# Root columns of five norms spread by one-pass products of high and low halves, in a two-layer diffusion block on one core

## The chip, the cores and the metric

The kernel runs on one core of a Trainium2 chip. The metric is the device time of one execution in microseconds (us). TensorE (PE) multiplies, and its weight loads (PEld) run beside its products. VectorE (DVE), ScalarE (ACT) and GpSimd (POOL) work elementwise, and SyncE (SP) issues the transfers (DMA).

## The reference

The input is 512 latent tokens and 256 context tokens of width 1024, all in float32. Two layers follow each other; each has a mixer (layer 0: Fourier groups and neighbourhood attention, layer 1: differential attention) and a squared-ReLU MLP of 4096 hidden units. Ahead of each of these four sub-layers, and once at the end, stands an RMS norm:

```
def rms_norm(x, g, eps=NORM_EPS):
    xf = x.astype(jnp.float32)
    y = xf * lax.rsqrt(jnp.mean(xf * xf, axis=-1, keepdims=True) + eps)
    return (y * g.astype(jnp.float32)).astype(x.dtype)

def modulate(x, g, shift, scale):
    return rms_norm(x, g) * (1.0 + scale) + shift
```

Shift, scale and gate come from the products of a condition vector with `w_mod` (1024 x 6144 for each layer).

## The kernel before, in words

Activations lie transposed: the 1024 features are 8 tiles of 128 partitions, the 768 tokens run along the free axis. Weights stream in as units of 128 x 1024 float32; ACT rounds each to float32r (`w_hi`, line 784), POOL makes the rest (`w_lo`, line 625), and PE takes every product as three one-pass products of halves: low by high, high by low, high by high (lines 1713 to 1715). The order of the work on each engine is written out by hand, and semaphores tie the engines together.

**A norm.** There are five, numbered i = 0 to 4, and each has two parts j: for i = 0, 1 and 2 the 512 latent tokens and the 256 context tokens, for i = 3 and 4 two halves of 256 latent tokens. ACT squares the features, DVE adds the eight tiles into `ssum`. `norm_sums` on PE (line 1764) sums `ssum` over the partitions, with `ssum` as weights and a column of ones, so that the sums stand as columns: one token for each partition, one column for each 128 tokens. ACT takes the square root into `stat` (line 822). `norm_root` on DVE takes the reciprocal (line 1280), and for each of the two or four columns writes a diagonal, `ident` times the column, into `diag` (line 1282). `norm_spread` on PE multiplies `diag` by a float32 matrix of ones (line 1771, one instruction in the source and two records in the trace), which leaves the row of roots, the same on all 128 partitions, in bank 6 + j. DVE multiplies it into the activations (line 1306), ACT and DVE make the high and low half of `h` (lines 836 and 1315), or ACT and POOL (line 643) for part 1.

**Where the spreads stand on PE.** For i = 1 to 4, part 0 is spread between two half units of the last projection (`tail`), part 1 for i = 1 to 3 inside the first three units of the next projection (`first_three`), and part 1 of i = 4 after the last product of the kernel; behind it come only the copy of the row, the last scaling and the output's transfers.

**The head.** PE starts with `hold(PAD, 7)`: 46 products of a float32r tile of ones with 512 columns of ones, whose result nobody reads. Then it works through this list, in order:

```
            half_mm(0)
            ...
            hold(3, 7)
            half_turn(0)
            ...
            norm_sums(0, 0)
            norm_sums(0, 1)
            half_mm(1)
            norm_spread(0, 0)
            norm_spread(0, 1)
            half_turn(1)
            hold(HOLD, 5)
            head_three(0, [(0, 0), (0, 1), (1, 0), (1, 1)])
```

`half_mm(m)` multiplies 512 modulation columns (`mod_big`, line 1918), each half of it after its own transfer; `half_turn(m)` turns the result into columns (line 1942), from which DVE makes the scale that the first `h` needs (lines 1474 and 1255). `head_three` are the first products of the projection. SP waits for the whole first `h` before it issues the next loads of weights.

Of the kernel before, what the change touches and what calls it, by code (L numbers as in the profile page):

```python
# [19 lines left out]
F32 = mybir.dt.float32  # L20
F32R = mybir.dt.float32r
ALU = mybir.AluOpType
# [3 lines left out]
P = 128  # L26
# [3 lines left out]
TOK = LAT + CTX  # L30
NT = TOK // P
# [28 lines left out]
MOD_VS = [2, 1, 1]  # L60
HPAIRS = HEADS // 2
HOLD = 12
PAD = 46
NTILES = HPAIRS * NT


# [20 lines left out]
def build(nc, t):  # L87

    ctx = ExitStack()
    with ctx:  # L90
        base = 16512

        def at(name, shape, dt, offset):
            return nc.alloc_sbuf_tensor_at(name, shape, dt, offset=offset)

        size = lambda *shape: int(np.prod(shape)) * 4
# [9 lines left out]
        scr = rest + 2 * size(TOK, KT)  # L106
# [9 lines left out]
        c_off = [con_at]  # L116

        def const(name, shape, dt=F32):
            o = c_off[0]
            c_off[0] += (size(*shape[1:]) + 31) // 32 * 32  # L120
            assert c_off[0] <= rest
            return at(name, shape, dt, o)

        ident = const("ident", [P, P])
        ones_r = const("ones", [P, P], F32R)
# [4 lines left out]
        cond = const("cond", [P, KT, 2])  # L130
        cact = const("cact", [P, KT, 2])
        eps_c = const("eps_c", [P, 2])
        stat = const("stat", [P, 64])
        modr = const("modr", [P, 2, 4])
        dft_at = c_off[0]
        dft_hi = const("dft_hi", [P, 256], F32R)
# [22 lines left out]
        tmp_a = at("tmp_a", [P, 2, TOK], F32, scr)  # L159
        tmp_b = at("tmp_b", [P, 2, TOK], F32, scr + size(2, TOK))  # L160
        ssum = at("ssum", [P, TOK], F32, scr + size(4, TOK))
        diag = at("diag", [P, NT, P], F32, scr + size(5, TOK))
        assert scr + size(6, TOK) <= mod_at


# [80 lines left out]
        ps = ctx.enter_context(nc.psum_tensor("ps", [P, 8, 512], F32))  # L246

        ones = ones_r[:].bitcast(F32)

        def sem(name):  # L250
            return ctx.enter_context(nc.semaphore(name))
# [32 lines left out]
        sq_summed = sem("sq_summed")  # L284
        norm_sum = sem("norm_sum")
        norm_sqrt = sem("norm_sqrt")
        norm_diag = sem("norm_diag")
        norm_rows = sem("norm_rows")
        t_made = sem("t_made")
        hh_made = sem("hh_made")  # L290
# [55 lines left out]
        c1 = sem("c1")  # L346
# [127 lines left out]
        def part(i, j):  # L474

            if i < 3:
                return (xl, 0, slice(0, LAT), slice(0, LAT)) if j == 0 else (xc, 1, slice(0, CTX), slice(LAT, TOK))
            half = slice(256 * j, 256 * j + 256)
            return xl, 0, half, half

        def width(s):
            return s.stop - s.start
# [694 lines left out]
        def _(dve):  # L1177
            st = Steps(dve, dsteps)
            V = nc.vector
            tt = V.tensor_tensor  # L1180
# [95 lines left out]
            def norm_root(i, j):  # L1276

                c0, c1 = part(i, j)[3].start // P, part(i, j)[3].stop // P
                dve.wait_ge(norm_sqrt, 2 * i + j + 1)
                st.wait(V.reciprocal(stat[:, 48 + c0:48 + c1], stat[:, 40 + c0:40 + c1]))  # L1280
                for c in range(c0, c1):
                    ins = V.tensor_scalar(diag[:, c], ident[:], stat[:, 48 + c:49 + c], None, ALU.mult)
                ins.then_inc(norm_diag, 1)

            def add_part(i, m, j):

# [195 lines left out]
            dve.wait_ge(consts_in, 16 * 6)  # L1482
            lam = lam_in[:].rearrange("p (a b) -> p a b", b=2)
            tt(lam_t[0:HD, 0:2], lam[:, :, 0], lam[:, :, 1], op=ALU.mult).then_inc(lam_ok, 1)
            V.tensor_reduce(group_sum[:], ident[:].rearrange("p (g v) -> p v g", g=4)[:, 0:2], AX.X, ALU.add).then_inc(group_ok, 1)
            V.tensor_scalar(subg[:, 1:2], subg[:, 0:1], 1.0 - LAM_INIT, None, ALU.mult)
            for m in range(3, 6):
# [46 lines left out]
            for m in range(4):  # L1534
                dve.wait_ge(u_hi_s, m + 1)
                tt(u_pair(u_lo, 4 + m // 2, m % 2), ps[:, V_BANK[m]], u_pair(u_hi, 4 + m // 2, m % 2).bitcast(F32),
                   op=ALU.subtract).then_inc(u_lo_s, 1)
            for p in range(5):
                if p < 4:
# [3 lines left out]
                    for e in range(2):  # L1543
                        tt(u_pair(u_sum, 2 * half + e, g), u_pair(u_sum, 2 * half + 1, g), ps[:, V_BANK[(5 + 2 * p) % 6]],
                           op=ALU.subtract if e else ALU.add).then_inc(u_sum_s, 1)
# [12 lines left out]
            for e in range(2):  # L1558
                for g in range(4):
                    dve.wait_ge(y_hi_s, 3 + 4 * e + (g | 1))  # L1560
                    tt(y_half(y_lo, g, e), y_ps(g, e), y_half(y_hi, g, e).bitcast(F32),
                       op=ALU.subtract).then_inc(y_lo_s, 1)
# [27 lines left out]
            for g in range(NTILES + 4):  # L1590
# [7 lines left out]
                if g >= 5 and g % 2:  # L1598
                    out_scaled((g - 5) // 2)

            dve.wait_ge(xr_in, 32)
            for i in range(4):
                u = FIRST["out0"] + i
# [104 lines left out]
        def _(pe):  # L1708
            mm = nc.tensor.matmul
# [57 lines left out]
            def norm_spread(i, j):  # L1767

                tok = part(i, j)[3]
                pe.wait_ge(norm_diag, 2 * i + j + 1)  # L1770
                mm(ps[:, 6 + j, 0:width(tok)], ones, diag[:].rearrange("p c q -> p (c q)")[:, tok],
                   start=True, stop=True).then_inc(norm_rows, 1)

            def tail(i, u, hi, lo, after_first=None):

# [168 lines left out]
                ins.then_inc(half_turned, 1)  # L1944

            pe.wait_ge(ones_ok, 1)
            def hold(n, bank):

                for _ in range(n):
                    mm(ps[:, bank].rearrange("p (c q) -> p c q", c=4), ones_r[:],  # L1950
                       ones_r[:].unsqueeze(1).broadcast_to([P, 4, P]), start=True, stop=True)

            hold(PAD, 7)
            half_mm(0)
            pe.wait_ge(lam_ok, 1)
            mm(ps[:, 6, 0:2], ones[0:HD, :], lam_t[0:HD, 0:2], start=True, stop=True).then_inc(lam_mm, 1)
# [82 lines left out]
            for g in range(4):  # L2039
                for j in range(4):  # L2040
                    c = slice(P * (j // 2), P * (j // 2) + P)
                    n = 4 + j % 2
                    ins = three(ps[:, 4 + g // 2, 256 * (g % 2):256 * (g % 2) + 256], (u_hi[:, n, g, c], u_lo[:, n, g, c]),
                                (w_hi[:, s, 256 * j:256 * j + 256], w_lo[:, s, 256 * j:256 * j + 256]), j == 0, j == 3)
            ins.then_inc(unit_done, 1)
            for e in range(2):
# [3 lines left out]
                for g in range(4):  # L2050
# [4 lines left out]
                    for j in range(4):  # L2055
                        c = slice(P * (j // 2), P * (j // 2) + P)
                        n = 2 * (j % 2) + e
# [393 lines left out]
```

## Time and profile before

| | us |
|---|---|
| median of three runs | 1615.65 (1615.43 to 1615.69) |
| the profiled execution's own time | 1615.17 |
| its span | 1613.4 |
| PE busy | 1593.0 (99%) |
| DVE, ACT, POOL busy | 983.9, 517.4, 617.5 |

The span is what the profiler records from the first to the last instruction. PE is busy in all but 20.4 us of it, and most of the time goes to the three products of lines 1713 to 1715. The granted clock of PE is 0.997 on the mean.

### The profile page before, as it was taken

What the parts mean: (1) busy time and instruction counts of PE and PEld (TensorE: products, weight loads), DVE (VectorE), ACT (ScalarE), POOL (GpSimd) and SP (SyncE); (2) the same over time, 40 slices, a digit from 0 to 9 for tenths busy, and PEclk for the clock granted to TensorE, in tenths of its full rate; (3) what the DMA queues carried; (4) which work ended last, traced back from release to release, by engine and by line L of the source; (5) the groups of instructions that cost most, each with busy time, mean ns of one, the idle gap of its engine ahead of it and who ended that gap; (6) DMA issues with size and microseconds to landing.
All of it is one profiled execution on the core that took longest, in us unless ns stands there. A gap on an engine that the chain in (4) does not pass through costs nothing.

```text
span 1613.4 us, 24201 instructions
## 1 busy us (share of the span) xinstructions
PE 1593.0 (99%) x9427; PEld 1432.4 (89%) x9427; DVE 983.9 (61%) x1316; ACT 517.4 (32%) x931; POOL 617.5 (38%) x402
## 2 busy tenths in 40 slices
PE   8999999999999999999999999999999999999997
PEld 5889988989999999999999888878889888888887
DVE  5697457258756764864784678229975825344354
ACT  4422466333211211211211512138864422222222
POOL 2422565335323322432331444244504644444441
PEclk9999999999999999999999999999999999999999
DMA  9473212213252234223332122110002322323221
GB/s 357 185 278 140 92 41 100 92 66 105 76 186 79 78 120 141 98 97 117 105 111 98 66 91 92 66 56 1 1 1 89 105 95 92 104 91 100 95 79 53
DMA packets 50334, 162.99 MB, mean 101 GB/s; under 512 B 6336, under 2 KB 8768, under 8 KB 46656
## 3 DMA queue, kind: packets, MB, share of 16 engines
q1 hardware_dynamic: 50240, 161.68, 28.8%
q8 instruction: 66, 1.08, 0.3%
q14 instruction: 28, 0.23, 0.0%
HBM read 158.78 MB, written 2.10 MB: 100 GB/s over the span
## 4 chain that ended last, share of the span: by engine, by line
PE 93%; DVE 2%; DMA 2%; issue 1%; ACT 1%; SPq 0%; POOL 0%; POOLq 0%; DVEq 0%; ACTq 0%
PE ps L1713 27%; PE ps L1714 26%; PE ps L1715 26%; PE ps L2239 3%; PE ps L2201 2%; PE ps L2228 1%; PE ps L2106 1%; PE ps L2094 1%; PE ps L2134 1%; PE ps L1918 1%; DMA mod_big<-w_mod_dram 1%; DMA mod_late<-w_mod_dram 1%; DMA raw<-units_dram 1%; PE ps L2129 1%; DVE h L1315 0%
## 5 line engine op out<-in xcount | busy, mean ns | idle before, releaser
L625 POOL TENSOR_TENSOR w_lo<-raw,w_hi 128x1024 fp32r<-128x1024 f32 (+1 forms) x235 | 483.3, 2068 | 838.3 <-ACT w_hi L784 838.1
L1713 PE MATMUL ps<-h,w_hi 128*128 128x384 f32 (+2 forms) x1176 | 409.8, 348 | 1.8 <-DVE h L1315 1.4
L1714 PE MATMUL ps<-h,w_lo 128*128 128x384 f32 (+2 forms) x1176 | 407.6, 347 | 0.0
L1715 PE MATMUL ps<-h,w_hi 128*128 128x384 f32 (+2 forms) x1176 | 407.3, 346 | 0.0
L784 ACT ACTIVATE w_hi<-raw 128x1024 fp32r<-128x1024 f32 x187 | 197.8, 1058 | 373.5 <-PE ps L1715 366.0
L1713 PE MATMUL ps<-hid_lo,w_hi 128*128 128x384 f32 (+2 forms) x800 | 277.6, 347 | 0.0
L1714 PE MATMUL ps<-hid_hi,w_lo 128*128 128x384 f32 (+2 forms) x800 | 276.5, 346 | 0.0
L1715 PE MATMUL ps<-hid_hi,w_hi 128*128 128x384 f32 (+2 forms) x800 | 276.4, 346 | 0.0
L1713 PEld LDWEIGHTS ps<-h,w_hi 128*128 128x128 f32 x1176 | 221.3, 188 | 25.3 <-issue 3.4
L1715 PEld LDWEIGHTS ps<-h,w_hi 128*128 128x128 f32 x1176 | 221.2, 188 | 16.4
L1714 PEld LDWEIGHTS ps<-h,w_lo 128*128 128x128 f32 x1176 | 221.3, 188 | 16.0
L1408 DVE SCALAR_TENSOR_TENSOR xl<-ps,mods,xl 128x384 f32<-128x384 f32 (+1 forms) x96 | 52.0, 570 | 241.1 <-PE ps L1715 240.7
L1713 PEld LDWEIGHTS ps<-hid_lo,w_hi 128*128 128x128 f32 x800 | 150.5, 188 | 12.0 <-DVE hid_lo L1423 1.5
L1714 PEld LDWEIGHTS ps<-hid_hi,w_lo 128*128 128x128 f32 x800 | 150.5, 188 | 10.5 <-issue 0.2
L1715 PEld LDWEIGHTS ps<-hid_hi,w_hi 128*128 128x128 f32 x800 | 150.5, 188 | 10.0
L891 ACT ACTIVATE tmp_a<-ps 128x384 f32<-128x384 f32 (+1 forms) x96 | 47.1, 526 | 314.2 <-PE ps L1715 294.5
L1423 DVE TENSOR_TENSOR hid_lo<-tmp_b,hid_hi 128x768 fp32r<-128x768 f32 (+1 forms) x64 | 133.8, 2091 | 2.2
L1419 DVE TENSOR_TENSOR tmp_b<-tmp_a 128x768 f32<-128x768 f32 (+1 forms) x64 | 74.2, 1160 | 96.1 <-ACT tmp_a L891 95.9
L1192 DVE SCALAR_TENSOR_TENSOR mod_acc<-mod_ring,cact,mod_acc 128x512 f32<-128x512 f32 x112 | 107.3, 978 | 16.5 <-DVE mod_acc L1192 13.8
L1130 ACT ACTIVATE aprob<-ps,stat 128x768 f32<-128x768 f32 x64 | 57.4, 898 | 7.2 <-DVE stat L1642 6.7
L1642 DVE TENSOR_REDUCE stat<-ps 128x1 f32<-128x768 f32 x64 | 57.9, 947 | 0.6 <-PE ps L2201 0.6
L1713 PE MATMUL ps<-w_lo,h 128*128 128x512 f32 x144 | 56.0, 389 | 0.0
(233 smaller groups left out, 2264.5 us busy)
## 6 DMA issues: line engine op xcount, KB each, us to landing
raw<-units_dram SPq DMA_DIRECT2D x187, 512.0 KB, 3.3
mod_ring<-w_mod_dram SPq DMA_DIRECT2D x96, 256.0 KB, 3.3
mod_big<-w_mod_dram SPq DMA_DIRECT2D x16, 1024.0 KB, 10.6
mod_late<-w_mod_dram SPq DMA_DIRECT2D x8, 1024.0 KB, 8.0
xl<-x_dram SPq DMA_DIRECT2D x2, 2048.0 KB, 8.4
bias<-bias_dram SPq DMA_DIRECT2D x8, 384.0 KB, 3.8
xc<-ctx_dram SPq DMA_DIRECT2D x2, 1024.0 KB, 10.4
out_dram<-out_t SPq DMA_DIRECT2D x16, 128.0 KB, 1.9
```

The source lines that it names most:

```text
L625: ins = nc.gpsimd.tensor_tensor(w_lo[:, s, sl], raw[:, s, sl], w_hi[:, s, sl].bitcast(F32), op=ALU.subtract)
L784: nc.scalar.activation(w_hi[:, s], raw[:, s], ACT.Copy).then_inc(hi_made, 1)
L1130: nc.scalar.activation(aprob[:, n % 3, i], scores_ps(n)[:, TOK * i:TOK * i + TOK], ACT.Exp, scale=-1.0, bias=stat[:, c:c + 1], accum_out=t ...
L1192: ins = V.scalar_tensor_tensor(out=mod_acc[:, v], in0=w, scalar=cact[:, k, v:v + 1], in1=mod_acc[:, v], op0=ALU.mult, op1=ALU.add)
L1408: ins = V.scalar_tensor_tensor(out=x, in0=ps[:, 2 * par + bank, cols], scalar=gate(layer, m, v, i), in1=x, op0=ALU.mult, op1=ALU.add)
L1419: ins = tt(tmp_b[:, i % 2, 0:n], tmp_a[:, i % 2, 0:n], tmp_a[:, i % 2, 0:n], op=ALU.mult)
L1423: tt(hid_lo[:, i, 0:n], tmp_b[:, i % 2, 0:n], hid_hi[:, i, 0:n].bitcast(F32), op=ALU.subtract).then_inc(hid_made, 1)
L1642: V.tensor_reduce(stat[:, c:c + 1], scores_ps(n)[:, TOK * i:TOK * i + TOK], AX.X, ALU.min).then_inc(m1, 1)
L1713: mm(out, a[0], b[1], start=start, stop=False)
L1714: mm(out, a[1], b[0], start=False, stop=False)
L1715: return mm(out, a[0], b[0], start=False, stop=stop)
L2239: ins = mm(out_ps, v1[:, c, P * h:P * h + P], aturn[m % 2][:, c], start=c == 0, stop=c == NT - 1)
```

## The change

`norm_root` makes no diagonals. It splits the reciprocal column into a float32r copy (high half, `stat_r` columns 54 on) and the difference (low half, columns 0 to 5), with one instruction each for all columns of the part. `norm_spread` takes, for each 128 tokens, two one-pass products: the column, repeated over 128 columns, as weights, times a float32r identity `ident_n`; low half first, then the high one on top. `ident_n` lies in the first half of `dft_hi` and is therefore copied twice by DVE: in the head, between the product of the lambda vectors and `group_sum`, and after the neighbourhood attention. The first hold becomes 82 products of 256 columns; the two later ones keep 512.

```
-PAD = 46
+PAD = 82
...
+        stat_at = c_off[0]
         stat = const("stat", [P, 64])
+        stat_r = at("stat_r", [P, 64], F32R, stat_at)
...
-        diag = at("diag", [P, NT, P], F32, scr + size(5, TOK))
+        ident_n = at("ident_n", [P, P], F32R, dft_at)
...
                 st.wait(V.reciprocal(stat[:, 48 + c0:48 + c1], stat[:, 40 + c0:40 + c1]))
-                for c in range(c0, c1):
-                    ins = V.tensor_scalar(diag[:, c], ident[:], stat[:, 48 + c:49 + c], None, ALU.mult)
-                ins.then_inc(norm_diag, 1)
+                st.wait(V.tensor_copy(stat_r[:, 54 + c0:54 + c1], stat[:, 48 + c0:48 + c1]))
+                tt(stat_r[:, c0:c1], stat[:, 48 + c0:48 + c1], stat_r[:, 54 + c0:54 + c1].bitcast(F32),
+                   op=ALU.subtract).then_inc(norm_split, 1)
...
             tt(lam_t[0:HD, 0:2], lam[:, :, 0], lam[:, :, 1], op=ALU.mult).then_inc(lam_ok, 1)
+            st.wait(V.tensor_copy(ident_n[:], ident[:]))
...
+            st.wait(V.tensor_copy(ident_n[:], ident[:]))
             dve.wait_ge(xr_in, 32)
...
-                pe.wait_ge(norm_diag, 2 * i + j + 1)
-                mm(ps[:, 6 + j, 0:width(tok)], ones, diag[:].rearrange("p c q -> p (c q)")[:, tok],
-                   start=True, stop=True).then_inc(norm_rows, 1)
+                pe.wait_ge(norm_split, 2 * i + j + 1)
+                for c in range(tok.start // P, tok.stop // P):
+                    o = ps[:, 6 + j, P * c - tok.start:P * c - tok.start + P]
+                    mm(o, stat_r[:, c:c + 1].broadcast_to([P, P]), ident_n[:], start=True, stop=False)
+                    ins = mm(o, stat_r[:, 54 + c:55 + c].broadcast_to([P, P]), ident_n[:], start=False, stop=True)
+                ins.then_inc(norm_rows, 1)
...
-            def hold(n, bank):
+            def hold(n, bank, c=4):
                 for _ in range(n):
-                    mm(ps[:, bank].rearrange("p (c q) -> p c q", c=4), ones_r[:],
-                       ones_r[:].unsqueeze(1).broadcast_to([P, 4, P]), start=True, stop=True)
-            hold(PAD, 7)
+                    mm(ps[:, bank, 0:P * c].rearrange("p (c q) -> p c q", c=c), ones_r[:],
+                       ones_r[:].unsqueeze(1).broadcast_to([P, c, P]), start=True, stop=True)
+            hold(PAD, 7, 2)
```

## Rows read from the trace of the kernel before

**Rows 1.** The page: busy time, share of the span, instructions

```profile
PE 1593.0 (99%) x9427; PEld 1432.4 (89%) x9427; DVE 983.9 (61%) x1316; ACT 517.4 (32%) x931; POOL 617.5 (38%) x402
```

**Rows 2.** Chain that ended last, head: start us, us, what (xcount)

```profile
24.46 2.48 PE ps L1771 x4
...
32.93 0.50 PE ps L1713
...
59.41 10.19 DMA raw<-units_dram
...
84.00 11.26 DMA mod_late<-w_mod_dram
```

**Rows 3.** Timeline of PE, head: start us, us, engine, line, operation [idle before, releaser]

```profile
2.00 12.55 PE L1950 MATMUL ps<-ones 128*128 128x512 f32 x46 [2.00 <-DVEq L1463]
15.16 1.06 PE L1918 MATMUL ps<-mod_big,cact_wide 128*32 128x512 f32 x8 [0.61 <-DMA mod_big<-w_mod_dram]
17.55 1.06 PE L1918 MATMUL ps<-mod_big,cact_wide 128*32 128x512 f32 x8 [1.33 <-DMA mod_big<-w_mod_dram]
...
21.88 2.58 PE L1918 MATMUL ps<-mod_big,cact_wide 128*32 128x512 f32 x16
...
27.59 3.01 PE L1950 MATMUL ps<-ones 128*128 128x512 f32 x12
```

**Rows 4.** Timeline of all engines, 2 to 6 us: the first constants

```profile
2.00 4.38 PE L1950 MATMUL ps<-ones 128*128 128x512 f32 x10 [2.00 <-DVEq L1463]
```

**Rows 5.** Windows of 1 us: PE, PEld, DVE, ACT, POOL busy, PEclk, DMA

```profile
22.00:23.00 1.00, 1.00 (x12) 0.29 (x13) 0.96 (x6) 0.25 (x1) 0.00 (x0) 1.00 1.04 426
23.00:24.00 1.00, 1.00 (x8) 0.00 (x0) 0.55 (x3) 0.22 (x1) 0.00 (x0) 0.51 1.03 410
...
26.00:27.00 1.00, 1.00 (x6) 0.69 (x4) 0.00 (x0) 1.00 (x1) 1.00 (x3) 0.79 1.01 422
```

**Rows 6.** Line 1771, its weight loads: duration ns minimum/median/maximum

```profile
L1771 PEld LDWEIGHTS ps<-diag,ones x20: 186/192/337, 24.4 to 1606.2; 128*128 128x128 f32 x20
```

**Rows 7.** Timeline of DVE, head

```profile
1.52 0.23 DVE L1460 CAST ones<-mod_acc 128x128 fp32r<-128x128 f32 x1
...
14.84 3.06 DVE L1266 TENSOR_TENSOR ssum<-ssum,tmp_b 128x768 f32<-128x768 f32 x3
...
23.10 0.48 DVE L1282 TENSOR_SCALAR diag<-ident,stat 128x128 f32<-128x128 f32 x2
```

**Rows 8.** Timeline of ACT, head: the fifth square

```profile
15.81 0.63 ACT L802 ACTIVATE tmp_b<-xl 128x512 f32<-128x512 f32 x1
```

**Rows 9.** Timeline of PE at 1201 us: eight products like the new ones

```profile
1201.09 0.39 PE L1715 MATMUL ps<-o_hi,w_hi 128*128 128x512 f32 x1
1201.32 0.22 PE L2291 MATMUL ps<-sub_rl,pick 128*128 128x128 f32 x1
...
1202.45 0.40 PE L1714 MATMUL ps<-o_hi,w_lo 128*128 128x512 f32 x1
```

**Rows 10.** Timeline of PE around the spreads of norms 1 and 3

```profile
350.55 0.28 PE L1715 MATMUL ps<-o_hi,w_hi 128*128 128x256 f32 x1
...
351.65 0.28 PE L1714 MATMUL ps<-f_hi,w_lo 128*128 128x256 f32 x1
...
1254.41 0.28 PE L1715 MATMUL ps<-h,w_hi 128*128 128x256 f32 x1
1254.91 0.70 PE L1771 MATMUL ps<-diag,ones 128*128 128x256 f32 x2 [0.23 <-DVE diag L1282]
```

**Rows 11.** Timeline of DVE at norm 3, part 1

```profile
1253.60 1.27 DVE L1282 TENSOR_SCALAR diag<-ident,stat 128x128 f32<-128x128 f32 x2
```

**Rows 12.** Timeline at the kernel's end

```profile
1605.35 0.17 DVE L1280 RECIPROCAL stat<-stat 128x2 f32<-128x2 f32 x1 [0.99 <-ACT stat L822]
1605.55 0.48 DVE L1282 TENSOR_SCALAR diag<-ident,stat 128x128 f32<-128x128 f32 x2
...
1606.09 0.70 PE L1771 MATMUL ps<-diag,ones 128*128 128x256 f32 x2 [1.07 <-DVE diag L1282]
```

More of the change, by code:

```diff
@@ L286, in build @@
         norm_sqrt = sem("norm_sqrt")
-        norm_diag = sem("norm_diag")
+        norm_split = sem("norm_split")
         norm_rows = sem("norm_rows")
```

## The prediction

> **What bounds the kernel now.** I read the page first: PE is busy 1593.0 of 1613.4 us [rows 1], so a change can bring something only where it takes work off PE, or in the 20.4 us in which PE waits. The chain that ended last says where waiting counts. In the head it runs through PE's spreads, 24.46 to 26.94, then on to the first product that waited for `h` at 32.93, and later through two loads of about 10 us each, at 59.41 and 84.00 [rows 2]. What is saved before 32.93 moves all of these, since SP issues the loads only when the first `h` is whole. From about 95 us on PE is full, so that there only PE's own time and its few idle stretches count, until the last product at 1603 us.
>
> Third the windows of the head: PE's granted clock is 1.00 up to 23 us, 0.51 between 23 and 24, and 0.79 between 26 and 27, that is half speed (1.2 GHz) from 23.0 to about 26.4 and 2.4 GHz outside it [rows 5]. Before it fell PE had waited 0.61 and 1.33 us for transfers [rows 3] and then run twenty products of one or two columns. The two norm spreads of the head, and the second half of the product before them, lie in this slow stretch. Fourth the timelines around each spread, for the price of one at full clock.
>
> **The change part by part.**
>
> *The spread on PE at full clock.* Old, 512 tokens: from the last product before it (350.55) to the second after it (351.65) are 1.10 us; two steps of 256 columns at 0.12 would be 0.24, so the spread costs 0.86 [rows 10]. A spread of 256 tokens costs half of that, 0.43. New: eight products of 128 columns with their own weights, which is just what PE does at 1201 us, also with a broadcast column as weights: from 1201.09 to 1202.45 are 1.36 us, less two steps of 512 columns at 0.23 is 0.90, or 0.112 each [rows 9]. So 512 tokens cost 0.90 and 256 tokens 0.45. Fewer passes, but each now pays for a weight load. Outside the head there are two spreads of 512 tokens and six of 256: 2 x 0.04 + 6 x 0.02 = 0.2 us more at most. The last of the six stands alone at the end and is counted there, so I take +0.15, between 0 and +0.2.
>
> *The spread on PE in the head.* Old: 2.48 us for 512 + 256 tokens [rows 2], against 0.86 + 0.43 = 1.29 at full clock. New: twelve products. At full clock 12 x 0.112 = 1.34. At half clock no row shows such a product. From below its step stays 0.112, if the weight load sets it and doesn't follow the clock; from above it doubles to 0.224. The nearest row is that of the old spread's weight loads: 192 ns in the median, 337 ns for one in the slow stretch, 1.75 times as long [rows 6]. By that a step is 0.196. Then in the 1.94 us from 24.46 to 26.4 ten products fit, the last two take 0.22, together 2.2 us: 0.3 saved. The ends are 2.3 us (step 0.224: nine slow, three fast, 0.15 saved) and 1.34 us (1.14 saved). I take -0.3, by the nearest row.
>
> The Trainium skill (TensorE: Matmul & The Clock Gate, section "LDWEIGHTS (loading the stationary operand)") puts a weight load at its number of columns divided by 1.2 GHz and names no dependence on the granted clock. At full clock the trace agrees, 0.107 us by the rule against 0.112 [rows 9]. At half clock the rule would leave the step at 0.107 and the head would save 1.2 us; the 337 ns speak against it, though a record's duration is no step.
>
> *The roots on DVE.* Four diagonals and a reciprocal become three small instructions. In the head nothing waits for them: the diagonals end at 23.58 [rows 7] and PE comes at 24.46, a cover of 0.88 us that only grows. Zero.
> At norm 3, part 1, the two diagonals took 1.27 us, because POOL was at work on the same memory, and end at 1254.87 [rows 11]; PE's spread began at 1254.91, though the product before it began at 1254.41 and would have let it start 0.12 later: 0.38 us lost [rows 10]. New: the copy starts at 1253.60, each small step takes 0.20 (reciprocal to next instruction at the end of the kernel: 1605.35 to 1605.55 [rows 12]), so the halves are ready at 1254.0, before PE. If one of them is stretched like one diagonal was (about 0.8), they are ready at 1254.7 and 0.2 is saved. I take -0.35, between -0.4 and -0.15. At the other parts of norms 1 to 4 PE doesn't wait; DVE gets up to 1 us free there, which nobody needs.
>
> *The end.* From the reciprocal (1605.35) to the end of the spread (1606.79) are 1.44 us [rows 12]. New: reciprocal, copy, difference at 0.20 each end at 1605.95, the weight load starts 0.05 later, and four products last from there some 0.65 (three steps of 0.112 and one product's length of 0.3): 1606.65. Saved 0.14; the copies and transfers behind it follow. Between 0 and -0.3.
>
> *The two copies of the identity.* The cast of a 128 x 128 tile takes 0.23, with its wait 0.29 [rows 7]. The second falls into DVE's idle time in the first output projection: zero. The first stands before DVE's third round of sums at 14.84. DVE is there a little behind ACT, and ACT's fifth square at 15.81 needs the buffer that the third round frees at about 15.8 [rows 7, 8], so both slip by up to 0.29. PE behind them is held by its three constants and the turn, and then by the transfer for the second half of `half_mm(1)`; I cost it at +0.05, between 0 and +0.3.
>
> *The first hold.* The 46 products last from 2.00 to 14.55 [rows 3]. Ten starts fall in the first 4.38 us, 0.40 to 0.43 apart, later ones are 0.24 apart (twelve in 3.01 [rows 3, 4]); so the array is at half speed up to about 5.9 us, though the clock's record shows nothing there. New: 256 columns need half of each step if columns bind, 0.21 and 0.12. Eighteen start by 5.9, the other 64 need 7.7 us: PE is free at 13.9 instead of 14.55. `half_mm(0)` waits for its transfer until 15.16 in both, so the time of the hold itself is hidden: zero, as long as 82 steps end before 15.1, and they do up to a step of 0.14. What remains is its effect on the clock: PE's wait before 15.16 grows from 0.61 to some 1.3 us.
>
> *Sum.* +0.15 - 0.3 - 0.35 - 0.14 + 0.05 = -0.6 us. The profiled execution took 1615.17 in all, 0.48 below the median of 1615.65, so the sum gives 1614.6 for it and 1615.05 as a median: 1615.0.
>
> **The rivals.**
>
> *B, the clock helps.* The slow stretch of the head goes away, or a step of 128 columns costs the same in it. For: the stretch follows PE's quiet work, and PE's waits move a little; the fast end of the bound above. Against: the small products before 21.88, after which the clock fell, stay as they are. Price: the second half of `half_mm(1)`: both halves took 2.58 where each takes 1.06 at full clock with overlap, so 0.7; and 1.14 for the spreads: 1.85 in place of the 0.3 of the forecast, so -2.15 in all: 1613.5.
>
> *C, the clock falls sooner (slower).* With the longer wait before 15.16 and the wait of 1.33 behind it, PE drops to half speed before 17.55. Then the second half of `half_mm(0)` takes 0.9 more, the three constants 0.6 more, and the twenty small products up to 1.8 more if each pays for its weight load (20 x 0.09). PE has no slack left here before `half_mm(1)` except what its transfer gives (some 0.9). It decides as soon as the clock is at half at 17.55. Price +1.5 to +3.3, less 0.9, and with the other terms at -0.3: +0.3 to +2.1, and up to +3 if that slack is used up by `half_mm(1)` running slowly too. I take +1.6: 1617.2. A like case is that the new spreads, with half the columns of the old, leave the clock low after 26.4: the turn and the twelve constants then cost about as much.
>
> *D, nothing moves.* The step at half clock is the full 0.224, the halves at norm 3 are stretched by POOL, and the weight loads cost 0.2: 1615.6.
>
> **How the numbers follow.** Forecast 0.5 (1614.3 to 1615.5), B 0.22, C 0.18, D 0.1. 0.2% of this kernel is 3.2 us, about what a measurement of it can tell from no change. The forecast and D lie wholly within it, B reaches 1612.4 (faster by more) only with something unseen, C passes 1618.9 only with both slow stretches. So faster 0.03, within 0.92, slower 0.05. The range goes from 1613.2 (B with 0.3 to spare) to 1617.2 (half of C).
>
> **What would show it right or wrong.** The chain's piece of line 1771 after 24.46: 2.2 us expected for twelve products in place of 2.48; 1.3 is B. The granted clock between 15 and 27 us: half speed from 23.0 to 26.4 again; a value under 1.00 before 20 is C. The first `head_three` product that waited at 32.93 should come 0.25 earlier. At norm 3 PE's idle time before the spread is gone. The spread of norm 1 should stretch its surroundings by 0.90 instead of 0.86. At the end, 1.3 us from reciprocal to the spread's end. The forecast is wrong if the first constants end after 15.1, or if the 32.93 moves by more than 1 us either way.

## The result, and the profile after

The changed kernel takes 1620.58 us (median of 20 runs, 1616.2 to 1622.2) beside 1615.65 (1614.1 to 1616.5): ratio 1.0027, 95% interval 1.0021 to 1.0033. It is slower by some 4.9 us where 0.65 less was forecast. The profiled execution took 1620.79, its span 1619.0, 5.6 more than before.

Two rows of the page after: each engine's busy time, share and instructions, then the DMA queue q8 with its packets, MB and share. The first answers to [rows 1]; q8 brings instructions and had 66 packets before:

```profile
PE 1598.2 (99%) x9495; PEld 1440.8 (89%) x9495; DVE 978.1 (60%) x1312; ACT 517.1 (32%) x931; POOL 616.3 (38%) x402
...
q8 instruction: 75, 1.23, 0.3%
```

There are 68 products more, 36 of the hold and 32 of the norms, and 68 weight loads. PE is busy 5.2 us longer, more than they can cost. And nine more pieces of instructions were fetched. PE's timeline of the head, which answers to [rows 3] and to the first of [rows 2]:

```profile
2.00 11.85 PE L1957 MATMUL ps<-ones 128*128 128x256 f32 x82 [2.00 <-DVEq L1465]
15.06 1.07 PE L1925 MATMUL ps<-mod_big,cact_wide 128*32 128x512 f32 x8 [1.21 <-DMA mod_big<-w_mod_dram]
17.46 1.06 PE L1925 MATMUL ps<-mod_big,cact_wide 128*32 128x512 f32 x8 [1.33 <-DMA mod_big<-w_mod_dram]
...
20.81 1.48 PE L1768 MATMUL ps<-ones,ssum 128*128 128x1 f32 x12
22.22 3.22 PE L1925 MATMUL ps<-mod_big,cact_wide 128*32 128x512 f32 x16
25.37 0.48 PE L1777 MATMUL ps<-ident_n,stat_r 128*128 128x128 f32 x1
...
27.78 0.41 PE L1778 MATMUL ps<-ident_n,stat_r 128*128 128x128 f32 x1
27.99 1.81 PE L1949 MATMUL ps<-group_sum,mod_acc 128*128 128x2 f32 x8
29.66 4.69 PE L1957 MATMUL ps<-ones 128*128 128x512 f32 x12
...
35.28 0.50 PE L1717 MATMUL ps<-h,w_hi 128*128 128x512 f32 x1 [0.23 <-DVE h L1317]
```

The hold ends at 13.85, as worked out. But `half_mm(1)` takes 3.22 instead of 2.58, the spreads 2.62 instead of 2.48, the twelve constants 4.69 instead of 3.01, and the first product that waited comes at 35.28 instead of 32.93. Windows of the same execution (PE busy, granted clock, DMA share, GB/s) answer to [rows 5]:

```profile
24.00:26.00 2.00, 2.00 (x11) 0.50 1.06 430
27.00:33.00 6.00, 6.00 (x22) 0.50 1.02 426
...
109.00:111.00 2.00, 2.00 (x8) 0.50 0.98 412
113.00:600.00 487.00, 486.98 (x3297) 1.00 0.29 100
600.00:767.00 167.00, 166.09 (x954) 1.00 0.35 117
```

The clock's record has half speed from 23.1 to 33.3 (before 23.0 to 26.4) and again from 108.4 to 111.8, where the kernel before ran at full clock. Ahead of the second stretch, and once in the loop of the first MLP (mlp0), PE stands idle in places where it did not before. (`early_lo` is the low half of sums that DVE makes of modulation products, and that PE adds up over the partitions.) Timeline of PE:

```profile
108.07 0.52 PE L1935 MATMUL ps<-early_lo,ones 128*128 128x512 f32 x1 [1.09 <-DVE early_lo L1227]
...
633.69 0.43 PE L1717 MATMUL ps<-h,w_hi 128*128 128x384 f32 x1 [0.91 <-issue]
```

The ledger says where the time goes. Each entry is the start of one ACT instruction less the start of the same instruction in the kernel before (us):

| at, before | 31.9 | 72.3 | 96.4 | 115.2 | 603 | 895 | 1243 | 1601 |
|---|---|---|---|---|---|---|---|---|
| changed kernel | +2.34 | +1.82 | +1.26 | +3.97 | +3.93 | +5.21 | +5.26 | +5.31 |
| narrow hold alone (e2) | +0.47 | +0.87 | +0.38 | +3.07 | +3.09 | +3.10 | +3.15 | +3.27 |
| norms alone (e1) | +1.19 | +1.22 | +1.34 | +1.41 | +1.41 | +1.41 | +1.43 | +1.44 |
| increments in the hold (e13) | -0.39 | -0.11 | -0.58 | +0.53 | +0.55 | +0.55 | +0.57 | +0.61 |
| increments after the head (e15) | -0.29 | -0.58 | -0.29 | -0.38 | -0.31 | +1.18 | +1.23 | +1.17 |
| short wide hold (e5) | +3.84 | +3.40 | +3.39 | +3.46 | +3.44 | +3.44 | +3.37 | +3.41 |
| norms 1 to 3 alone (e14) | -0.90 | -0.98 | -0.92 | -0.94 | -0.94 | -0.94 | -0.92 | -1.04 |

The changed kernel loses its time at three places: before 32 us, between 105 and 115, and in the loop between 603 and 895. A row is one execution. The runs of one kernel differ by 1.6 us (e15) to 6 us (changed), mostly with the clock: of the kernel before, 56 runs at a mean clock of 0.997 have a median of 1615.0 and 38 at 0.996 one of 1615.7. Of the changed kernel's 20 runs 11 were at 0.994 or lower (1620.5 and more), four at 0.997 (median 1617.3) and two at 0.996 (1616.9). So some 1.2 to 2.3 us are lost at equal clock, and the rest comes with a lower clock.

### The profile page after: what moved, and what is told of

Its sections match the earlier page's. It is cut to its first block, busy times and chain, and to the rows that moved or that the text cites. A ratio compares the mean times of both kernels' runs of the same rounds, so it can differ in the third digit from the quotient of the medians.

```text
span 1619.0 us, 24333 instructions
## 1 busy us (share of the span) xinstructions
PE 1598.2 (99%) x9495; PEld 1440.8 (89%) x9495; DVE 978.1 (60%) x1312; ACT 517.1 (32%) x931; POOL 616.3 (38%) x402
## 3 DMA queue, kind: packets, MB, share of 16 engines
q8 instruction: 75, 1.23, 0.3%
## 4 chain that ended last, share of the span: by engine, by line
PE 92%; DVE 3%; DMA 1%; issue 1%; ACT 1%; SPq 0%; POOL 0%; POOLq 0%; DVEq 0%; ACTq 0%
PE ps L1717 26%; PE ps L1719 26%; PE ps L1718 26%; PE ps L2246 3%; PE ps L2208 2%; PE ps L2235 1%; PE ps L2113 1%; PE ps L2101 1%; PE ps L2141 1%; DVE early_acc L1216 1%; DMA mod_big<-w_mod_dram 1%; PE ps L1925 1%; PE ps L2136 1%; DMA raw<-units_dram 1%; DVE h L1317 0%
## 5 line engine op out<-in xcount | busy, mean ns | idle before, releaser
L1718 PEld LDWEIGHTS ps<-hid_hi,w_lo 128*128 128x128 f32 x800 | 150.5, 188 | 10.2
L1719 PEld LDWEIGHTS ps<-hid_hi,w_hi 128*128 128x128 f32 x800 | 150.5, 188 | 10.1
## 6 DMA issues: line engine op xcount, KB each, us to landing
xc<-ctx_dram SPq DMA_DIRECT2D x2, 1024.0 KB, 10.1
```

The source lines that it names most:

```text
L1718: mm(out, a[1], b[0], start=False, stop=False)
L1719: return mm(out, a[0], b[0], start=False, stop=stop)
```

## The experiments

I went on with three theories. Theory F (fetch): what costs is where PE's instruction stream stands, that is, at which instruction each piece of it ends. It is fetched in pieces of 16 KB over queue q8. Rows of the DMA view (packets, MB, share of 16 engines), first the changed kernel from 18 to 20 us, then the kernel before from 23 to 25, which has none from 18 to 20:

```profile
q8 instruction: 1, 0.02, 3.4%
```

```profile
q8 instruction: 1, 0.02, 3.3%
```

One piece takes about 1.1 us on one DMA engine (3.4% of 16 engines in 2 us). 36 more products, each with a weight load, are 72 more instructions; the first piece fetched within the span (the expectations call it the second) comes at 19.0 instead of 23.6, and the third after it at 80.9 instead of 89.0. Theory H: the hold itself, its end, columns or product size, leaves the head at half clock for longer. Theory S: the sparse spreads of the head do.

| run | edit | median us (range, runs) | ratio, 95% | q8 |
|---|---|---|---|---|
| e1 | changed, old hold | 1615.2 (1613.3 to 1619.1, 11) | 1.0003 [0.9994, 1.0012] | 66 |
| e2 | before, new hold | 1618.04 (1615.4 to 1621.1, 11) | 1.0017 [1.0008, 1.0026] | 66 |
| e3 | changed, norm 0 by diagonals | 1618.77 (1617.2 to 1621.8, 8) | 1.0024 [1.0013, 1.0034] | 66 |
| e4 | before, norm 0 in halves | 1616.62 (1614.1 to 1618.6, 11) | 1.0009 [1.0, 1.0019] | 66 |
| e5 | changed, hold of 41 x 512 | 1618.86 (1615.6 to 1621.4, 11) | 1.002 [1.0011, 1.0029] | 66 |
| e6 | before, hold of 92 x 256 | 1620.29 (1616.7 to 1621.3, 6) | 1.0031 [1.0019, 1.0044] | 75 |
| e7 | e1, 72 increments in the hold | 1619.05 (1617.0 to 1622.4, 9) | 1.0025 [1.0015, 1.0035] | 75 |
| e8 | e1, 72 increments after the head | 1618.21 (1616.5 to 1622.1, 11) | 1.0024 [1.0015, 1.0033] | 75 |
| e9 | e1, eight constants in the head's gaps | 1616.61 (1615.5 to 1619.2, 11) | 1.0009 [1.0, 1.0018] | 66 |
| e10 | changed, 144 increments after the head | 1618.32 (1615.8 to 1620.5, 11) | 1.0022 [1.0013, 1.0031] | 67 |
| e11 | changed, four constants at 107 us | 1620.66 (1616.9 to 1622.3, 6) | 1.0029 [1.0017, 1.0041] | 75 |
| e12 | before, the eight constants of e9 | 1615.82 (1615.2 to 1619.9, 11) | 1.0008 [0.9999, 1.0017] | 66 |
| e13 | before, 72 increments in the hold | 1618.02 (1615.8 to 1619.0, 11) | 1.0017 [1.0008, 1.0026] | 66 |
| e14 | norms 1 to 3 in halves, old hold | 1615.69 (1613.9 to 1617.7, 11) | 1.0006 [0.9997, 1.0015] | 66 |
| e15 | before, 117 increments after the head | 1617.08 (1615.9 to 1617.5, 11) | 1.0012 [1.0003, 1.0021] | 75 |

The kernel before had 1615.1 to 1615.3 beside them. An increment is a `sem_inc` on a semaphore that nobody waits for: one instruction of PE's queue and no product. q8 counts the pieces fetched. The medians of e4, e5, e6, e8, e9, e10 and e12 lie outside every range that was given for them.

**The parts alone (e1 to e4).**

```
e1, of the changed kernel           e2, of the kernel before
-PAD = 82                           -PAD = 46
+PAD = 46                           +PAD = 82
-            hold(PAD, 7, 2)        -            hold(PAD, 7)
+            hold(PAD, 7)           +            hold(PAD, 7, 2)
```

> The changed kernel with the old first hold (46 constants of 512 columns); all five norms in halves. Theory S (the head's twelve products of 128 columns leave too little streaming in the slow stretch, so the clock stays at half from 23 to 33 us): slow as the changed kernel, 1618 to 1621 us, granted clock at half for 6.8 to 10.2 us in one stretch from 23. Theory H (the first hold's earlier end does it): about 1615 to 1616, half speed only from 23.0 to 26.4.

> The kernel before with the new first hold alone (82 constants of 256 columns); norms by diagonals. Theory S: 1615 to 1616 us, as before. Theory H: 1618 to 1621, with a longer stretch at half speed in the head or one that begins before 20 us.

The norms alone cost nothing that can be measured; the hold alone costs 2.9 us (1618.04 beside 1615.19). The profiled run of e1 has the long stretch at half clock and is 1.4 us behind, yet the median of the 11 runs is that of the kernel before. One of the windows of e1 reads

```profile
27.00:33.00 6.00, 6.00 (x20) 0.50 1.01 422
```

So one trace showed a loss that is not the typical one. e3 and e4 put the diagonals back for norm 0 alone (`if i == 0:` four and two `tensor_scalar`, and the old product), or keep only norm 0 in halves (`if i > 0:`, old hold):

> The changed kernel, but norm 0 (the head's) spread by diagonals as before; the copies of the identity and the 82 constants stay. Theory S: the clock is back at 26.4 us and the time is 1615.3 to 1616.5 (the copy of the identity still moves the head by 0.3). Theory H: 1618 to 1621. A third theory (I, the copy of the identity ahead of the sums delays PE by 0.3 and so shifts dense work out of the stretch): 1617 to 1620.

> The kernel before with norm 0 alone in halves (with the copy of the identity in the head), the other four norms by diagonals, the old first hold. Theory S: within 1 us of the changed kernel, 1618 to 1621: the whole loss comes from the head. If norms 1 to 4 carry some of it (PE's own time and the end of the kernel), this kernel is 0.3 to 0.6 us faster than e1. Theory H: 1615 to 1616.

With the hold new and the head's spreads old (e3) 3.6 us are lost; with the spreads new and the hold old (e4) 1.4, with an interval down to nothing. So theory S carries at most the smaller part. e3 is no clean test of it against the changed kernel, since it also has 66 pieces instead of 75. Something remains for S: a stretch of 10.2 us at half clock in the head stands in four of nine profiles with the head's spreads in halves (changed, e1, e10, e11) and in none of eight with diagonals.

**The shape of the hold (e5, e6).** e5: `PAD = 41` and `hold(PAD, 7)` in the changed kernel. e6: `PAD = 92` and `hold(PAD, 7, 2)` in the kernel before.

> The changed kernel with its first hold of 41 constants of 512 columns in place of 82 of 256: the same number of columns and (within 0.5 us) the same end of the hold, but 82 fewer instructions of TensorE (41 weight loads and 41 products). Theory F (what costs is where TensorE's instruction stream stands: the extra products of the hold move its 16 KB fetches, the second one from 24 us to 19): the second fetch comes back to 24 to 25 us, the second half of half_mm(1)'s weights lands a microsecond earlier (by 22.6 us), no idle place of 1.1 us at 107 us, 66 fetches in all, and the median is that of the norms alone, 1615.2 (1614.6 to 1616.2). Theory H (the shorter or less dense hold itself leaves the head colder): as the changed kernel, 1619 to 1621.

> The kernel before with 92 constants of 256 columns in place of 46 of 512: all columns of the old hold, with 92 more instructions of TensorE. Theory F: the second fetch moves from 23.6 to about 18 us and the later ones with it, half_mm(1)'s second half lands a microsecond later, TensorE waits 1 us for DVE's early_lo at 107 us: median 1617.5 to 1618.5, as with 82 of 256 in the kernel before (1618.0). Theory H (fewer columns): nothing is lost, 1615.2 (1614.6 to 1616). If 256-column products are in themselves the reason, this one loses too, so only together with the stream shifted alone does it tell the two apart.

e6 has all columns of the old hold and loses 5.0 us: fewer columns are not the reason. That is more than F gave for it, since its 92 instructions also bring the refetching of the loop (75 pieces; see below). e5 misses F's number, but by another mechanism. Its hold ends at 13.15, PE waits longer, and the clock is at half from 15.6 to 29.2 (timeline of PE, then a window):

```profile
15.08 1.49 PE L1925 MATMUL ps<-mod_big,cact_wide 128*32 128x512 f32 x8 [1.94 <-DMA mod_big<-w_mod_dram]
17.48 1.94 PE L1925 MATMUL ps<-mod_big,cact_wide 128*32 128x512 f32 x8 [0.91 <-DMA mod_big<-w_mod_dram]
```

```profile
16.00:29.00 13.00, 12.09 (x53) 0.50 1.02 419
```

That is the mechanism of rival C, at more than its price (+3.8 at 32 us), and nine of its 11 runs have a mean clock of 0.994 or lower, as the profiled one. After 32 us nothing more is lost: no idle place at 107, no refetching, as F said. At waits of 1.21 to 1.52 us at the same place (changed, e2, e3, e10) it did not happen in any profile. So H holds too, for a hold that is shorter still.

**The stream alone, no product changed (e7, e13).**

```
-            hold(PAD, 7)
+            for k in range(PAD):
+                hold(1, 7)
+                for _ in range(2 if k < 26 else 1):
+                    pe.sem_inc(passed, 1)
```

> The norms in halves with the old hold of 46 constants of 512 columns, and between these constants 72 bare semaphore increments of TensorE's queue that nobody waits for: its instruction stream is then as long, from the head on, as the changed kernel's, while the products are those of the old hold. Theory F: the loss of the changed kernel comes back, 1618.5 to 1621, with fetches at about 18.7, 44, 61, 80.5 and 111 us, the idle place at 107 us, and 75 fetches in all with a stall of 0.9 us in mlp0's loop. Theory H (the products): as the norms alone, 1615.2 (1614.6 to 1616.2). The increments may stretch the hold; it has 0.5 us before the first weights of the modulation land.

> The kernel before with nothing but 72 bare semaphore increments in TensorE's queue between the constants of the first hold: the instruction stream of the head and after stands as in the kernel before with 82 constants of 256 (1618.0), no product is another, and mlp0's loop isn't refetched (66 fetches). If the stream's place in the head is what costs there: fetches at 18.8 and 81 us, the idle place of 1.1 us at 107 us, and 1617.5 to 1618.5. If the 256-column products are it: 1615.2 (1614.6 to 1615.8), also with an idle place at 107 us.

e13 is the deciding run: with the kernel before's products, all of them, it takes 1618.02, as the narrow hold alone takes 1618.04. The end of the hold isn't the reason either: it ends at 15.12 in e13 and at 13.46 in e2. e7 does the same beside the norms in halves: 1619.05, with 75 pieces, which is most of what the changed kernel loses. Rows of e13's profile, PE, PE and DVE:

```profile
23.50 1.06 PE L1919 MATMUL ps<-mod_big,cact_wide 128*32 128x512 f32 x8 [0.67 <-DMA mod_big<-w_mod_dram]
...
106.20 0.50 PE L1929 MATMUL ps<-early_lo,ones 128*128 128x512 f32 x1 [1.09 <-DVE early_lo L1226]
```

```profile
104.92 1.23 DVE L1226 TENSOR_TENSOR early_lo<-early_acc,acc_hi 128x1024 fp32r<-128x1024 f32 x1
```

and the same two instructions before:

```profile
105.68 0.50 PE L1928 MATMUL ps<-early_lo,ones 128*128 128x512 f32 x1
```

```profile
104.40 1.23 DVE L1225 TENSOR_TENSOR early_lo<-early_acc,acc_hi 128x1024 fp32r<-128x1024 f32 x1
```

Before, DVE ends `early_lo` at 105.63 and PE asks for it at 105.68: no slack, and no wait. In e13 DVE is 0.5 later and PE 0.6 earlier. PE is earlier because a transfer of `mod_late` lands sooner (modulation weights, in pieces of 1 MB). SP issues its second piece at 84.58 instead of 84.00 [rows 2], and yet PE reads it at 94.73 instead of 95.31: the transfer takes 10.1 us instead of 11.3. The fetch that lay within it at 89 us now comes at 80. The shares of the chain of waits from 55 to 110 us tell the same of the kernel before and of the changed one:

```profile
by line: DMA mod_late<-w_mod_dram 20.5%; DMA raw<-units_dram 18.5%; issue 14.3%; DVE early_acc L1214 7.7%; PE ps L1713 7.3%; PE ps L1714 7.0%; PE ps L1715 7.0%; POOL h L643 3.8%; SPq L501 2.4%; PE ps L1918 1.9%; SPq L514 1.6%; ACT f_hi L956
```

```profile
by line: DVE early_acc L1216 29.1%; issue 17.4%; DMA raw<-units_dram 15.2%; DVE early_lo L1227 8.3%; POOL h L645 5.2%; DVE f_lo L1514 2.8%; ACT f_hi L958 2.7%; DVE acc_hi L1226 2.4%; DVE modr L1245 2.2%; DVE early_acc L1241 2.2%; ACT w_hi L
```

The transfer is gone from the chain and DVE's sums are in its place. These sums lose 0.66 to 0.70 us between 72 and 76 us against before, in the changed kernel and in every experiment but e1, e5, e14 and e15, where it is 0.2 or less. An earlier fetch goes with this too. Rows of ACT, POOL and DVE, of the kernel before and then of e13:

```profile
67.03 1.06 ACT L784 ACTIVATE w_hi<-raw 128x1024 fp32r<-128x1024 f32 x1 [4.17 <-DMA raw<-units_dram]
70.77 5.17 POOL L625 TENSOR_TENSOR w_lo<-raw,w_hi 128x1024 fp32r<-128x1024 f32 x2 [0.20 <-ACT w_hi L784]
72.42 4.07 DVE L1214 SCALAR_TENSOR_TENSOR early_acc<-mod_big,cact,early_acc 128x512 f32<-128x512 f32 x2
```

```profile
67.83 1.06 ACT L785 ACTIVATE w_hi<-raw 128x1024 fp32r<-128x1024 f32 x1 [5.35 <-DMA raw<-units_dram]
68.97 7.53 POOL L626 TENSOR_TENSOR w_lo<-raw,w_hi 128x1024 fp32r<-128x1024 f32 x3 [11.79 <-ACT w_hi L785]
72.32 4.73 DVE L1215 SCALAR_TENSOR_TENSOR early_acc<-mod_big,cact,early_acc 128x512 f32<-128x512 f32 x2
```

Before, the fetch comes at 67.1, between the landings of two weight units (67.0 and 69.6), and POOL pauses between them. In e13 it comes at 62.7, the first unit lands only at 67.8 and the second 1.28 us behind it; POOL works without a pause, so that 1.37 us of it lie beside DVE's first sum instead of 0.72, and that sum takes 1.92 us instead of 1.27. The two landings are 1.28 to 1.29 us apart in all 12 profiles that lose the 0.7, and 2.2 to 2.6 us apart in the five that don't. That is a match of times in 17 profiles; no run moved this fetch alone.

PE's idle time of 1.0 to 1.25 us stands in eight profiles (changed, e2, e3, e6, e7, e9, e10, e13), just those that lose the 0.7 and in which this piece of `mod_late` takes 9.3 to 10.2 us, where it takes 11.1 to 11.4 in the others (e11 is the ninth of them and fills the gap). In four of them the clock falls behind it (changed, e2, e3, e7), which costs another 1.6 (e2: +0.36 at 105 us, +3.07 at 115; e9, where it did not fall: -0.39 and +0.67).

The profile of e13 shows only 0.6 us of the 2.9: it is the fastest of the 11 runs, at a mean clock of 0.998. Its seven runs at 0.996 have a median of 1618.0, beside 1615.7 for the kernel before at 0.996. So most of its loss isn't a lower mean clock, and where in the kernel the slower runs lose it no trace shows. And no run puts the head's fetches back into their old places by adding instructions; only e5 does it by taking some away.

**The loop (e8, e10, e15).**

```
             def three(out, a, b, start, stop, last=None):
+                called[0] += 1
+                if 440 < called[0] <= 440 + n:
+                    pe.sem_inc(passed, 1)
```

> The norms in halves with the old hold (as the norms alone, 1615.2), and 72 bare semaphore increments in TensorE's queue between products of the stretch from about 360 to 400 us: from there on the instruction stream stands where the changed kernel's does, ahead of it where the norms alone stood. Theory F splits into a part in the head and a part in mlp0's loop. If the loop's part is what the changed profile shows (75 fetches instead of 66, an idle place of about 0.9 us at the start of an iteration), this kernel has it and nothing else: 75 fetches, the stretch from norm 1 to norm 2 longer by 0.8 to 1.3 us, no idle place at 107 us, median 1616.0 to 1616.5. If refetching costs nothing, 1615.2.

> The changed kernel with 144 bare semaphore increments between products from about 360 to 440 us, so that mlp0's loop starts at another place within its 16 KB pieces, one where kernels without refetching had it. Theory F: 66 or 67 fetches, none between 613 and 765 us, the stretch from norm 1 to norm 2 back to 526.3 us, and 1.2 us less than the changed kernel: 1619.0 to 1619.8. If the place of the loop is not the cause of the refetching, 75 fetches and 1620.6 as before.

> The kernel before with 117 bare semaphore increments between products from about 360 to 420 us, so that mlp0's loop starts at the place within its 16 KB pieces where the changed kernel's does; head, norms and products are as before. If the place of the loop alone is a cause: 75 fetches, 1.0 us or more between norm 1 and norm 2, and the median 1616.5 to 1618.3 (the pairs measured so far differ by 2.3 to 3.0, their profiled runs by 1.0). If it needs the halved norms: 66 fetches and 1615.2.

All four pairs with and without refetching differ the same way: e15 against the kernel before +2.0, e8 against e1 +3.0, e6 against e2 +2.3, changed against e10 +2.3 (the intervals of the last two pairs overlap). The sizes expected for e8 and e10, taken from profiles, were half of what came or less. In e10 the time from norm 1 to norm 2 is that of before again. The DMA view from 612 to 766 us of the kernel before, then of e15, and e15's PE rows:

```profile
q8 instruction: 1, 0.02, 0.0%
```

```profile
q8 instruction: 10, 0.16, 0.5%
```

```profile
629.04 0.44 PE L1719 MATMUL ps<-h,w_hi 128*128 128x384 f32 x1 [0.50 <-issue]
...
631.82 0.43 PE L1719 MATMUL ps<-h,w_hi 128*128 128x384 f32 x1 [0.42 <-issue]
```

PE runs the loop's body twice; its last product before the jump back begins at 628.2 us. Before, there is one fetch in this window. With the stream 92 to 111 instructions further on (e6 92, e8 101, changed and e7 104, e11 and e15 111; the trace shows a few increments less than were written) there are ten, four of them between 622 and 633 us. With 72 (e2) there are two, with 88 (e3) and with 242 (e10) one. The Trainium skill (Runtime: NRT & Kernel Launch, section "Instruction fetch mechanics") gives PE 128 KiB refilled in 16 KiB blocks of 256 instructions, calls the cost of a block boundary mostly hidden, and says that a taken branch whose target lies outside the current window of two pages forces a fetch. The traces agree on 16 KB a piece. With its figures the loop's 1,591 instructions (776 products, a weight load each, 39 others) are an estimated 6.2 of 8 blocks, which touch seven or eight depending on where they begin; the kernel before jumps back over all of them with one fetch in 154 us, so a window of two pages doesn't fit its trace. Nor is the cost mostly hidden here: e13 only moves boundaries and takes 2.9 us more, e15 brings the refetching and takes 2.0.

**Filling gaps (e9, e12, e11).**

```
e9, e12: in half_mm, ahead of the second wait    e9, e12: between norm_sums(0, 1) and half_mm(1)
+ if m == 0 and j == 1:                          + hold(3, 5)
+     hold(5, 7)
e11: in early_mm, ahead of pe.wait_ge(mod_summed, m - 3)
+ if m == 5:
+     hold(4, 6)
```

> The norms in halves with the old hold, and constants of 512 columns in two idle stretches of TensorE: five between the halves of half_mm(0) (idle 1.33 us there) and three ahead of half_mm(1), whose second half waits for its weights anyway. If the clock of the head falls for want of work in these stretches, the stretch at half clock at 23 us gets shorter or goes: per microsecond that it is shorter, half a microsecond is won in half_mm(1), the spreads and turn(1), up to 1.5 us: 1613.7 to 1615. If the clock falls all the same, the three constants cost up to 0.3 us at full clock: 1615.2 to 1615.8.

> The kernel before (diagonals, 46 constants of 512) with the eight constants of the filled head alone: five between the halves of half_mm(0) and three ahead of half_mm(1). If the fill keeps the clock up in the head, as the profile of the filled norms in halves showed, the stretch of 3.4 us at 23 us goes and h is ready 0.3 to 1.0 us sooner; what that is worth depends on DVE's early chain and the transfer of mod_late: 1614.3 to 1615.3. If the shift of the instruction stream by 16 instructions matters, or TensorE then waits for early_lo at 107 us, 1616 to 1617 as with the norms in halves.

> The changed kernel with four constants of 512 columns (0.92 us) written to a free bank just ahead of early_mm(5), where TensorE waits 1.1 us for DVE's early_lo. The theory that the 3.4 us at half clock that follow are what makes this place dear (1.7 of its 2.6 us): the idle place shrinks to 0.2 us, no stretch at half clock at 108 us, and the median falls by 1 to 1.7 us, to 1619.0 to 1619.6. If the clock falls there for another reason, nothing changes: 1620.6.

In e9's profile the clock stays up in the head (windows):

```profile
16.00:22.00 6.00, 5.80 (x42) 1.00 1.00 421
22.00:34.00 12.00, 10.28 (x62) 1.00 1.02 418
```

That it was the fill isn't shown: e12's profile has no slow stretch in the head either, but neither have those of e8, e13 and e14, which have no fill. And nothing was won: neither median is below that of the kernel before. In e12's profile the head is 0.90 ahead at 62 us and 0.06 at 96, with DVE's 0.7 and the transfer of `mod_late` in between; in e9's the wait for `early_lo` takes it. e11 is a miss. In its profile the idle place and the half-speed stretch at 108 are gone, 115 us is reached 1.0 later than 105 instead of 2.7, but the loop's refetching took 2.4 there and the median stayed.

**The best of the parts (e14).** Diagonals for norms 0 and 4, halves for 1 to 3, old hold (`if i in (0, 4):` as in e3).

> The old hold of 46 constants of 512 columns, norm 0 in the head and norm 4 at the end spread by diagonals as before, norms 1 to 3 by the products of halves; the copy of the identity is still made. Theory F: a shift of 16 to 20 instructions moves no fetch into another place, norms 1 to 3 cost 0 to 0.1 us more on TensorE, the clock of the head is that of the kernel before: 1615.1 to 1615.6, so no gain. If the spreads at full clock were worth what was predicted for norm 3's second part (0.35 us), 1614.8.

No gain in the median, though the profiled run is 1.0 us ahead at the end. No version beats the kernel before; e1 equals it.

## Why the prediction was wrong

**The first hold: "hidden: zero".** This step failed. Its time was right (13.85 against 13.9, the wait 1.21 against 1.3), and of its effects I listed only the one on the clock. Its 72 more instructions I priced as products, not as a stream. Shown by e13: 72 instructions at that place cost 2.9 us in the median with no product behind them. With the 2.0 of the refetching (e15) that is the 4.9 us of the changed kernel; that the two add up so exactly is luck, since each is uncertain by more than 1 us.

**The added products at full clock: "+0.15".** The products were right: at norm 1 the eight of them cost 0.89 (1.13 from neighbour to neighbour, less two steps of 0.12) against 0.90 worked out. But norms 0 and 1 put 32 instructions ahead of the loop, which with the hold's 72 pass the place from which it is refetched; neither alone does (e1, e2). Shown by e15 (+2.0) and, with overlapping intervals, e10: about 2 us. None of the prediction's rivals had this or the hold's stream.

**The spread in the head: "-0.3".** Mis-sized. From 25.37 to 27.99 are twelve steps of 0.218: at half clock the step is 0.213, nearly the upper bound of 0.224, not 0.196. The weight load's duration, from which I took it, was no step. The Trainium skill's rule (TensorE: Matmul & The Clock Gate, "LDWEIGHTS (loading the stationary operand)") would have left 0.107; these rows don't agree. Beyond that the clock stayed low after 26.4 in several profiles with the new spreads (changed, e1, e10, e11, not e4, e8, e9), the like case under rival C. In the median the new spreads of the head cost near zero in e1 and 1.4 in e4, whose interval reaches down to nothing.

**Norm 3: "-0.35".** Rows of DVE and PE, which answer to [rows 11] and [rows 10]:

```profile
1258.88 0.51 DVE L1283 CAST stat_r<-stat 128x2 fp32r<-128x2 f32 x1
1259.42 0.65 DVE L1284 TENSOR_TENSOR stat_r<-stat,stat_r 128x2 fp32r<-128x2 f32 x1
```

```profile
1259.68 0.28 PE L1719 MATMUL ps<-h,w_hi 128*128 128x256 f32 x1
1260.13 0.33 PE L1777 MATMUL ps<-ident_n,stat_r 128*128 128x128 f32 x1 [0.17 <-DVE stat_r L1284]
```

Both small instructions are stretched (0.54 and 0.58 apart), where I had allowed for one. From the product before to the spread are 0.45 instead of 0.50: 0.05 saved. With two columns an instruction took as long beside POOL as with 128, some 0.6 us (1.27 for two in [rows 11]); that POOL is the reason is argued from its being at work then, not tested.

**The end: "-0.14".** It answers to [rows 12] (DVE, then PE):

```profile
1610.66 0.17 DVE L1282 RECIPROCAL stat<-stat 128x2 f32<-128x2 f32 x1 [0.99 <-ACT stat L824]
...
1611.28 0.48 PE L1777 MATMUL ps<-ident_n,stat_r 128*128 128x128 f32 x1 [0.95 <-DVE stat_r L1284]
...
1611.98 0.41 PE L1778 MATMUL ps<-ident_n,stat_r 128*128 128x128 f32 x1
```

DVE's part is 0.12 shorter, as worked out. But the clock had fallen at 1610.3, and the four products end 1.73 after the reciprocal's start, not 1.44: 0.3 lost.

**The identity copy: "+0.05".** `half_mm(1)` begins 0.34 later, just beyond its bound of 0.3; in e1 0.26.

Rival B came in part in e9's profile (no slow stretch), and its gain was not kept, because `mod_late` and DVE's sums set the time behind it. D's terms fit the norms alone (e1). "What is saved before 32.93 moves all of these" holds where the fetches keep their places: the shift of the head stays to the end in e1, e5 and e14 (ledger), and not in the changed kernel. "From about 95 us on PE is full" fails for the changed kernel, which idles at 107 and 633.

Open: why the head's stream costs 2.9 us in the median and 0.6 in e13's profile; why refetching costs 2 to 3 us in the median and 0.8 to 1.5 in all profiles but e11's; and whether the half clock behind the idle place at 107 matters in the median (e11 speaks against it, in six runs).

## What to carry to other kernels

Count added and removed instructions of an engine's queue, not only their time: in this long unrolled stream they moved each later fetch, and at a loop of 1,591 instructions they brought refetching. The row q8 of the page (66 or 75 pieces) shows the second at a glance, and bare increments in the queue test both without touching the work. One profile is one draw: judge a clock effect by many runs and their mean clocks before it is called the cause.

## What the runs showed of the hardware

- A product of 128 columns with its own 128-column weights takes 0.213 us a step at 1.2 GHz and 0.112 at 2.4 GHz.
- A semaphore increment on PE's queue lasts 51 ns and the next follows 0.15 us after it; with 72 of them among 46 constants the hold lasted 13.1 to 13.2 us (e13, e7), without them 12.4 to 13.6 (before, e1, e4, e8, e14, e15).
- A fetch of 16 KB of instructions takes about 1.1 us on one DMA engine (0.9 to 2.2 over all traces). A 1 MB transfer on which the chain hangs took 11.3 us with such a fetch in it and 10.1 without (before, e13).
- The loop of 1,591 instructions on PE was refetched with 92 to 111 instructions more ahead of it (e6 to e8, e11, e15, changed), and not with 88 (e3), 72 (e2, e13) or 242 (e10).
- A DVE sum of 128 x 512 took 1.27 us with 0.72 us of POOL's work beside it, and 1.92 us with 1.37 (before, e13).
- A stretch at half clock followed a wait of 1.94 us (e5) and did not follow waits of 1.21 to 1.52 us at the same place (changed, e2, e3, e10).
